# Delta rule in two chunks of 128 tokens with one more doubling level, and the columns of z computed ahead of those of v

## The reference

```
qkv, z, a, b = split(h @ w_in, [3072, 4096, 4104])      # 8 heads of 128
q, k, v = split(silu(causal_dwconv4(qkv)))
q, k = l2norm(q), l2norm(k);  beta = sigmoid(b)
g = -exp(a_log) * softplus(a + dt_bias)
o = gated_delta_rule_chunked(q, k, v, g, beta)           # S_t = a_t S_{t-1} (I - b_t k_t k_t^T) + b_t v_t k_t^T
o = rmsnorm(o, o_norm) * silu(z);  return o @ w_out

# inside the chunked rule, per chunk, with decay = exp(gcum_i - gcum_j) for j <= i:
amat = I + strict_lower(kb @ k^T * decay)                # kb = k * beta
u, w = solve(amat, [v * beta, kb * exp(gcum)])
qk = q @ k^T * decay
v_new = u - w @ S;  o = (q * exp(g)) @ S + qk @ v_new
S = S * exp(g_last) + (k * exp(g_last - g))^T @ v_new
```

## Time and profile before

| | |
|---|---|
| median of 3 runs | 3000.39 us (2999.1 to 3005.29) |
| the profiled execution | 3005.67 us, its span 3003.9 us |
| PE busy | 2781.3 us, 93% of the span |
| DVE busy | 1868.6 us, 62% |
| ACT busy | 1411.5 us, 47% |
| mean granted TensorE clock | 0.952 |
| DMA | 450.11 MB, 150 GB/s on average |

### The profile page before, as it was taken

One profiled execution on the slowest core, in us unless ns is written; L12 is line 12 of the kernel. 1 busy time (PEld: TensorE's weight loads), 2 busy tenths in 40 slices (PEclk: granted clock), 3 DMA queues, 4 the chain that ended last, 5 costly groups with the idle time before them and its releaser, 6 DMA issues. The chain is left out here.

```text
span 3003.9 us, 49268 instructions
## 1 busy us (share of the span) xinstructions
PE 2781.3 (93%) x21174; PEld 2676.6 (89%) x21174; DVE 1868.6 (62%) x2412; ACT 1411.5 (47%) x1896; POOL 0.2 (0%) x4
## 2 busy tenths in 40 slices
PE   7998989999986898999999999869998899999998
PEld 7998889999976878999888999759987899989998
DVE  5657656666567426666655766867556376665664
ACT  5444545454564234544445445444454354445443
POOL 0000000000000000000000000000000000000000
PEclk9999999999988879999999999979998799999999
DMA  6554436655523114455444464115643155553464
GB/s 204 182 189 131 158 112 194 192 186 184 189 92 96 56 63 148 151 186 193 154 153 137 155 203 148 64 58 190 198 134 105 57 193 187 174 168 123 153 200 134
DMA packets 129001, 450.11 MB, mean 150 GB/s; under 512 B 20112, under 2 KB 20368, under 8 KB 128528
## 3 DMA queue, kind: packets, MB, share of 16 engines
q1 hardware_dynamic: 128784, 446.97, 46.3%
HBM read 445.47 MB, written 1.44 MB: 149 GB/s over the span
## 5 line engine op out<-in xcount | busy, mean ns | idle before, releaser
L248 PE MATMUL B<-R,WH 128*128 128x256 f32 x10432 | 2100.1, 285 | 86.4 <-DVE R L933 39.4
L248 PEld LDWEIGHTS B<-R,WH 128*128 128x128 f32 x10432 | 1698.1, 192 | 103.9 <-DVE R L933 29.7
L867 DVE TENSOR_TENSOR WL<-SL,WH 128x1024 fp32r<-128x1024 f32 x836 | 1010.6, 1223 | 793.9 <-ACT WH L1816 792.7
L248 PE MATMUL B<-R,WL 128*128 128x256 f32 x4480 | 1269.9, 283 | 0.0
L1816 ACT ACTIVATE WH<-SL 128x1024 fp32r<-128x1024 f32 x836 | 865.7, 1052 | 594.7 <-PE B L248 475.8
L248 PEld LDWEIGHTS B<-R,WL 128*128 128x128 f32 x4480 | 863.0, 193 | 0.0
L248 PE MATMUL B<-RB,WH 128*128 128x256 f32 x1984 | 556.2, 280 | 0.0
L248 PE MATMUL B<-RB,WL 128*128 128x256 f32 x1728 | 481.9, 279 | 0.0
L248 PEld LDWEIGHTS B<-RB,WH 128*128 128x128 f32 x1984 | 374.4, 189 | 0.4 <-DVE WL L867 0.2
L248 PEld LDWEIGHTS B<-RB,WL 128*128 128x128 f32 x1728 | 324.8, 188 | 0.0
L248 PE MATMUL B<-PG 128*128 128x256 f32 (+6 forms) x752 | 158.9, 371 | 9.0 <-DVE PG L958 2.1
(11 more groups left out here) (283 smaller groups left out, 1595.2 us busy)
## 6 DMA issues: line engine op xcount, KB each, us to landing
SL<-in_w SPq DMA_DIRECT2D x836, 512.0 KB, 4.0
CP<-in_cp SPq DMA_DIRECT2D x5, 768.0 KB, 4.9
X<-in_xT SPq DMA_DIRECT2D x2, 512.0 KB, 6.7
PG<-in_mem SPq DMA_DIRECT2D x1, 1024.0 KB, 10.9
out<-X SPq DMA_DIRECT2D x1, 1024.0 KB, 3.9
PK<-in_pk SPq DMA_DIRECT2D x1, 598.5 KB, 3.8
dn_y<-PG SPq DMA_DIRECT2D x1, 256.0 KB, 2.2
PG<-dn_y SPq DMA_DIRECT2D x16, 16.0 KB, 1.9
```

The costliest lines, as they stand in the source:

```text
L248: return p.matmul(o, left, right, start=first, stop=final, skip_group_check=True)
L867: v.tensor_tensor(WL[t % NSPL][:, :], SL[t % NRAW][:, :], WH[t % NSPL][:, :].bitcast(F32), ALU.subtract).then_inc(s_lo, 1)
```

## The change

The delta rule takes chunks of 128 tokens, so that a chunk fills a 128x128 tile. The running sums and masks cover 128 tokens. `invert` has three levels (16 to 32, 32 to 64, 64 to 128), the last without `dy`. There are two chunks; the state of the first is only copied (`dkv`, by ACT into H), so `add_keys` on DVE, the clearing of the state, w of the first chunk and the keys for the end of the second are gone. All matmuls of the chunks are 128x128.

The columns of z come at x = 64 to 95 and those of v at x = 96 to 127, and the work beside the blocks is placed anew: `cumulate` and `drw` ahead of the first `squares`, `dkk` and `dlt` six blocks later, `dkt` at 86 to 89, `invert` at 101 to 124, the turned values, the solve and the chunks between the steps of `xv1a` and `xv1b`. The squares of the l2 norms have four places in PG[9] in place of two. The small DMAs go out eight at a time.

```diff
-            rows += [("dn.k", 8, 4, 1), ("dn.q", 8, 4, 1), ("dn.v", 8, 4, 1), ("dn.z", 8, 4, 1), ("xv1a", 8, 1, 2), ("xv1b", 8, 1, 2), ("xk1a", 8, 2, 1),
+            rows += [("dn.k", 8, 4, 1), ("dn.q", 8, 4, 1), ("dn.z", 8, 4, 1), ("dn.v", 8, 4, 1), ("xv1a", 8, 1, 2), ("xv1b", 8, 1, 2), ("xk1a", 8, 2, 1),
...
-        SUMMED = (24, 27, 36, 44, 52, 66, 71, 79)
+        SUMMED = (33, 35, 38, 46, 54, 68, 72, 80)
...
-                    mm(bk[:, :], ONES[:, :], PG[9][:, hc(j % 2)]).then_inc(s_small, 1)
+                    mm(bk[:, :], ONES[:, :], PG[9][:, hc(j % 4)]).then_inc(s_small, 1)
...
-                    if lev == 4:
+                    if lev == 0:
                         p.wait_ge(s_dn_y[1], 128)
-                    four(("dy", lev, q), lambda i: sl(YT, q, i), lambda i: sl(M1, q, i))
+                    if lev < 2:
+                        four(("dy", lev, q), lambda i: sl(YT, q, i), lambda i: sl(M1, q, i))
...
-                    if x == 24:
+                    if x == 26:
                         cumulate()
                     if x in SUMMED:
                         squares(SUMMED.index(x))
-                    if 28 <= x < 32:
+                    if 29 <= x < 33:
                         p.wait_ge(dn_wide.sem, dn_wide["g"])
-                    if 62 <= x < 66:
+                        four(("drw", x - 29), lambda i: sl(WIDE, x - 29, i), lambda i: U)
+                    if 68 <= x < 72:
                         p.wait_ge(dn_qk.sem, dn_qk["k"])
-                    if 66 <= x < 70:
+                        four(("dkk", x - 68), lambda i: part(2048, 4 * (x - 68) + i), lambda i: part(2048, 4 * (x - 68) + i))
+                    if 72 <= x < 76:
+                        freed(("dkk", x - 72))
+                        turned(("dlt", x - 72), lambda i: sl(L, x - 72, i))
+                    if 86 <= x < 90:
+                        turned(("dkt", x - 86), lambda i: part(2048, 4 * (x - 86) + i))
...
-                    if 100 <= x < 104:
-                        turned(("dkt", x - 100), lambda i: part(2048, 4 * (x - 100) + i))
-                    if 106 <= x < 122:
-                        invert((x - 106) // 8 + 4, (x - 106) % 8)
-                    if 104 <= x < 108:
-                    if 122 <= x < 126:
-                        q = x - 122
-                        four(("duu", q), lambda i: sl(YT, q, i), lambda i: sl(VB, q, i))
-                        four(("dwt", q), lambda i: sl(KB, q, i), lambda i: sl(YT, q, i))
-                    if x == 126:
-                        read_out(0)
-                    if x == 127:
-                        add_keys(0)
...
+                    if 101 <= x < 125:
+                        invert((x - 101) // 8, (x - 101) % 8)
+
+                def solve_values(q):
+                    freed(("dyt", 2, q))
+                    freed(("dvt", q))
+                    four(("duu", q), lambda i: sl(YT, q, i), lambda i: sl(VB, q, i))
+
+                def solve_keys(q):
+                    freed(("dyt", 2, q))
+                    freed(("dkt", q))
+                    four(("dwt", q), lambda i: sl(KB, q, i), lambda i: sl(YT, q, i))
+
+                def add_keys(q):
+                    freed(("duu", q))
+                    four(("dkv", q), lambda i: sl(KN, q, i), lambda i: sl(UU, q, i))
+
+                def less_state(q):
+                    freed(("dwt", q))
+                    freed(("dkv", q - 2))
+                    four(("dws", q), lambda i: sl(WT, q, i), lambda i: sl(ZT, q - 2, i))
+
+                def read_out(q):
+                    freed(("duu", q))
+                    freed(("dkq", q))
+                    bk = small(("do", q))
+                    if q >= 2:
+                        freed(("dws", q))
+                        p.wait_ge(dn_qg.sem, dn_qg["qg"])
+                    for i in range(4):
+                        o = bk[:, i * 128:(i + 1) * 128]
+                        if q >= 2:
+                            mm(o, sl(ZT, q - 2, i), part(0, 4 * q + i), True, False)
+                        t = mm(o, sl(UU, q, i), sl(QT, q, i), q < 2, True)
...
-                    if k == 1:
-                        less_state(1)
-                    if k == 3:
-                        read_out(1)
-                        add_keys(1)
-                    if k == 6:
-                        less_state(2)
+                    if k < 2:
+                        solve_keys(2 + k)
+                    if 3 <= k < 7:
+                        q = (0, 2, 1, 3)[k - 3]
+                        p.wait_ge(dn_act.sem, dn_act[9 + 2 * (q % 2)])
+                        turned(("dvt", q), lambda i: part(4096, 4 * q + i))
+                    if k == 5:
+                        solve_values(0)
+                    if k == 7:
+                        solve_values(1)
                 for j, k in gemm("xv1b", R67, R67, 0, 2048):
-                    if k == 0:
-                        read_out(2)
-                        add_keys(2)
-                    if k == 3:
-                        less_state(3)
-                    if k == 5:
-                        read_out(3)
+                    if k in (0, 1):
+                        solve_values(2 + k)
+                        add_keys(k)
+                    if k in (2, 3):
+                        read_out(k - 2)
+                        less_state(k)
+                    if k in (5, 6):
+                        read_out(k - 3)
...
-                    if x in (33, 37, 41, 45):
-                        masked(x // 4 - 8)
-                    if x == 53:
+                    if x in (36, 41, 44, 49):
+                        masked((36, 41, 44, 49).index(x))
+                    if x == 57:
                         normalize("k", BIG[:, 2048:4096], PG[4], 1.0)
...
+                    if 79 <= x < 87:
+                        eliminate(2 * x - 158)
+                        if x < 86:
+                            eliminate(2 * x - 157)
...
+                    if x == 90:
                         normalize("q", BIG[:, 0:2048], PG[5], 128.0 ** -0.5)
...
+                    if 91 <= x < 95:
+                        keys(x - 91)
...
+                    if 102 <= x < 126:
+                        invert((x - 102) // 8, (x - 102) % 8)
+                    if x == 100:
+                        v.tensor_tensor(Q3, Q3, q4(ER[:, 1024:2048]), ALU.mult).then_inc(dn_qg.sem, dn_qg.give("qg"))
...
-                    if 15 < x < 96 and x % 8 == 7:
-                        taken(x // 8)
-                        conv(x // 8)
-                    if x >= 96 and x % 8 == 7:
-                        scaled_to("dn.z", x // 8 - 12, BIG, 6144)
+                    if x % 8 == 7 and 64 <= x < 96:
+                        scaled_to("dn.z", x // 8 - 8, BIG, 6144)
+                    elif x % 8 == 7 and x > 15:
+                        g = x // 8 - (4 if x > 96 else 0)
+                        taken(g)
+                        conv(g)
...
-                for q in range(4):
-                    freed(("duu", q))
                 for j, k in walk("xv1a"):
-                    if k == 2:
-                        less_state(1)
-                    if k == 4:
-                        add_keys(1)
-                    if k == 7:
-                        less_state(2)
+                    if k > 3:
+                        values((0, 2, 1, 3)[k - 4])
                 for j, k in walk("xv1b"):
-                    if k == 1:
-                        add_keys(2)
-                    if k == 4:
-                        less_state(3)
+                    if k in (3, 4):
+                        less_state(k - 1)
...
-                    if x in (29, 37, 45, 58, 62, 70, 77, 92, 94, 102):
-                        gate((29, 37, 45, 58, 62, 70, 77, 92, 94, 102).index(x) + 2)
-                    if x in (48, 82):
+                    if x in (30, 38, 46, 60, 62, 71, 110, 118, 126):
+                        gate((30, 38, 46, 60, 62, 71, 110, 118, 126).index(x) + 2)
...
+                    if x in (78, 92, 95, 101):
+                        silu_of("dn.z", (78, 92, 95, 101).index(x), Z)
...
+                    if k == 1:
+                        gate(11)
+                    if k in (2, 3):
+                        solved("dwt", k, WT)
+                    if k == 6:
+                        solved("duu", 0, UU)
+                solved("duu", 1, UU)
                 tok_to("xv1a", 0, lambda tb: PG[1][:, tb * 1024:tb * 1024 + 512], False)
                 for j, k in walk("xv1b"):
-                    if k == 1:
-                        output(2)
-                    if k == 6:
-                        output(3)
-                        for n in range(4):
-                            freed(("do", n))
-                    if k > 5:
-                        squared(2 * k - 12)
-                        squared(2 * k - 11)
+                    if k in (1, 2):
+                        solved("duu", k + 1, UU)
+                        solved("dkv", k - 1, H)
```

(86 more changed lines are left out.)

163 lines of the change are left out of this document (47 added, 116 removed).

## The result

The changed kernel took 2955.12 us (median of 4 runs, 2945.37 to 2963.82) and the kernel before, on the same chip, 2999.74 (2998.75 to 3005.29): ratio 0.9847, 95% interval 0.9809 to 0.9884. The forecast was 2959. The interval of the ratio lies clear of 1. The profiled execution of after took 2960.28 us, its span is 2958.5. Its runs follow the granted clock of the whole span (0.959, 0.959, 0.966 and 0.964 in the runs of 2960.28, 2963.82, 2945.37 and 2949.97 us), so a difference of 10 us between two kernels is read from stages and not from the total.

The account below looks back on a forecast made before the run. TensorE, busy 93% of the span, bounds the kernel; only its waits, slow clock and own instructions can be saved. 4.4 + 5.0 + 3.4 + 28.7 = 41.5 us off 3005.7 gives 2964.2 profiled, median 2959; range 2939 to 2979.

Parts of the forecast that it names:

- Stage 4: x = 128 to 159: small products and waits removed, 44.7 us instead of 73.4, a gain of 28.7 us.
- The allowance of 4 us for the clock: x = 128 to 159: 4 us added to the walked 40.7 because nothing guarantees the high clock.
- Stage 1: x = 0 to 75: x = 76 starts at 920.1 instead of 924.5, a gain of 4.4 us.
- The wait at x = 68: Before `dkk`: TensorE waits some 7 us, until `normalize` of k ends on DVE behind ScalarE's exponentials.
- Stage 2: x = 76 to 100: 36.3 us instead of 41.3, a gain of 5.0 us.
- the predicted bank wait: At x = 89 the fourth `dkt` waits 11.1 us for the bank that only `keys(0)` empties.
- Stage 3: x = 101 to 127, with the inversion: 67.8 us instead of 71.2, a gain of 3.4 us.
- The ring of 2.17 us: In the inversion: two 2.17 us waits of the earlier trace, cited against many evacuation waits, not counted in the walk.
- rival B: In the inversion each of 32 `four` waits for its own evacuation: gain 23.8 us less, 2983 us; chance 0.14.
- A: Larger gain, 60.5 us, to 2940: neither 4 us allowance needed and the x = 89 wait gone; chance 0.13.
- C: Slower, 3019 us: TensorE and DVE alternate fully in Stage 3, which takes 128.1 us; chance 0.04.
- D: No change: waits move but add up the same, Stage 4's saving is lost to clock below 0.75; chance 0.03.

Follow-up runs that it names:

- the sorted kernel: Kernel before the change, with `read_out` doing the state's eight products first, then the chunk's own eight: 2988.31 us against 2997.76, ratio 0.9975.
- the nine traces: Profiled executions of the changed kernel and its follow-ups with nothing changed in x = 0 to 75, which took 99.5 to 101.8 us.
- the repeat: The changed kernel measured once more with no edit: 2960.7 us, ratio 0.9862 to the kernel before.
- the seven traces: Profiled executions of the changed kernel and its follow-ups with nothing changed in x = 101 to 127, which took 71.0 to 76.5 us.
- cols_back: The changed kernel with the columns of v, their gates, taps and convolution back ahead of z: 2955.5 us, ratio 0.9845 to the kernel before.

## Why the prediction was right, and where it was not

**Stage 4, the large term, held** (28.7 forecast, 30.3 found). Its three parts can be told apart. Alternating the forms: 8.0 us by the sorted kernel, some 6 of it the 42 changes fewer at full clock (16 products in 3.65 us, from 1069.26 to 1072.91, instead of 5.8, three times), the rest where the clock is low (0.43 us apiece sorted, 0.62 in alternation). The prediction read the 0.36 us as the price of a small product; it is the price of one in alternation, and alone it is 0.22 to 0.24. Halves at the price of wholes: split in two, the 40 whole products of after take 8.0 to 10.2 us more. And the clock, 0.75 over 73.4 us, which is up to 18 us. These overlap and are not a sum. The allowance of 4 us for the clock was not needed for the clock, which was 1.00: 40.7 walked, 43.1 found. Of the 2.4 us between, 1.9 are waits: the two forecast came (about 1; 1.04 and 1.32), and with them 0.89, 0.46 and 0.16. The Trainium skill's "TensorEngine Tiling (Array Packing)", Theoretical Speedup, would have made the gain 12.5 us smaller; the measured 30.3 and the 0.24 us of a 64-row product speak against applying it here, where consecutive products read the same rows. The same page of the Trainium skill says (Key Properties) that a change of the tiling mode drains the engine; the 0.42 us of alternating products, against 0.24 of 64-row ones alone, agree.

**Stage 1** (4.4 forecast, 6.4 found; 4.8 to 7.1 over the nine traces). The new wait at x = 31 came (5.9 forecast, 5.75), and x = 36 started 47.3 us after x = 0 in the one run and 48.8 in the other, with 48.9 before: as today, as forecast. The wait at x = 68 was 6.32 (about 7 forecast), but in front of the `squares` there, which ScalarE releases, and not of the `dkk` behind it. ScalarE is late there by its own queue, as its timeline shows: no idle time between the exponentials, the upper halves and a table load:

```profile
884.95 2.43 ACT L2105 ACTIVATE PG<-PG,RT 128x128 f32<-128x128 f32 x8
...
891.85 1.04 ACT L1769 ACTIVATE WH<-SL 128x1024 fp32r<-128x1024 f32 x1
892.91 1.28 ACT L2080 ACT_TABLE_LOAD   x1
894.20 0.63 ACT L2080 ACTIVATE BIG<-BIG 128x512 f32<-128x512 f32 x1
894.86 0.63 ACT L2085 ACTIVATE PG<-BIG 128x512 f32<-128x512 f32 x1
```

The norm of k ends at 896.2, the same moment within 0.6 us, so the forecast's cause was one of two that meet. The 3.5 us before the fourth `dkk` were 1.73.

**Stage 2** (5.0 forecast, 5.5 found; the trace of after is the shortest of nine, most give 3.0 to 3.6). The wait before the fourth `dkt` is the predicted bank wait, 8.92 us (up to 10.8 in the others) instead of 11.1. The elimination starts 4.7 us after x = 76 (920.72 to 916.0); the forecast had 6.0 (926.1 to 920.1).

**Stage 3 is the step that failed** (a gain of 3.4 forecast, a loss of 2.4 found, 4.9 in the repeat; over the seven traces from a gain of 0.6 to that loss). The sentence "Three waits of 4.0, 4.1 and 3.3, and 5.8 us of slow clock behind them, give 63.8 us" counted the right three waits and no others. The ring of 2.17 us, which I had seen in the earlier trace rows and used only as evidence against rival B, comes twice in the new stage too, and the walk left it out; opening it gave 4.9 to 10.4 us for its 4.3 of waiting. With it opened the stage took 66.1, near the 63.8 walked. The slow clock was mis-sized as well: TensorE was busy for 57.8 us with what the walk priced at 46.7, where 5.8 were put down for the clock. My allowance of 4 us covered part of both by luck. The waits of the stage add up to 16.1 us, where before they were 9.4.

**Rivals.** A did not come: the wait at x = 89 stayed. B did not: five waits, not 32. C would need 109 us in stage 3; it took 74.0. D did not: the stages gained 39.8 us. That the sum came within 2 us of the stages (39.8 for 41.5) is the stages' errors cancelling: +2.0, +0.5, -5.8 and +1.6. It is luck of the run, too: by the trace of the repeat the same four stages gained 33.9.

**Open.** What makes the clock fall in stage 4 of before is not settled. It falls at 1049.6, 1077.0 and 1097.4. The first and the third fall come 2.1 and 1.4 us after the end of a wait of 2.5 us, the second after 9.8 us in which TensorE was busy all the time; all three lie in the products of `read_out`. Of the things that differ in after, neither halves of columns, nor of rows, nor alternation alone did it in after (all 1.00), and sorting did not cure it. Products halved in both ways were not tried in after, nor were two halves of rows side by side in the array. That the waits of 2.5 us are part of the cause isn't tested either; the stage after has none above 1.32, while cols_back kept clock 1.00 behind one of 2.52. What the new places and the eight DMAs together did, apart from the chunks, no run shows. The 3.5 us gained behind x = 160 lie within the spread of the totals.

## What to carry to other kernels

Here small f32 products of one stream cost by the piece, not by the size: make them 128 by 128, and where two sizes must stay, sort them by form. A piece of elementwise work that is moved to another stage takes its wait along; look at what is queued behind it there, and cut it in two if a bank of TensorE's stands behind it. A short wait that recurs is not noise: follow it once around. If it closes into a ring between queues, swap the two instructions of which the front one waits and the back one is ready.

## What the runs showed of the hardware

A 128x64 product took 0.22 us, a 64-row one 0.24 and a 64x64 one about 0.23 (the estimate above), against 0.20 for 128x128; alternating 64 and 128 rows took 0.42 apiece at granted clock 1.00. TensorE's granted clock fell to 0.50, the 1.2 GHz level, with TensorE 100% busy, in the kernel before:

```profile
1067.20:1077.00 9.80, 9.80 (x57) 8.13 (x57) 3.44 (x4) 2.03 (x3) 0.00 (x0) 1.00 0.24 74
1077.00:1087.00 10.00, 10.00 (x33) 8.50 (x34) 2.25 (x8) 0.60 (x1) 0.00 (x0) 0.50 0.10 40
```

and, behind a wait of 2.50 us that ended at 1047.55:

```profile
1053.00:1061.00 8.00, 8.00 (x30) 7.01 (x31) 0.00 (x0) 0.00 (x0) 0.00 (x0) 0.50 0.00 0
```

Ahead of both falls were 64x64 and 128x64 products in turn. So a busy engine is no proof of a fast one. What a wait costs beyond its length differs from run to run: over seven traces of one stage with the same five waits (16.1 us) the granted clock was 0.82 to 0.90 and the stage took 71.0 to 76.5 us; 4.3 us of waits removed gave 4.9 to 10.4. And two waits of 2.17 us cost no clock at all in cols_back (1.00).
